# A transformer kernel on one core: the order of the dilated rounds, gates by tanh, normings of the sink layer on two engines, and a tile ahead of the norm roots

## Time and profile before

| | |
|---|---|
| median of three runs | 2550.37 us |
| profiled execution, device time | 2553.59 us |
| its span | 2551.8 us |
| PE busy | 2441.9 us, 96% |
| DVE, ACT, POOL busy | 1234.9, 984.5, 217.1 us |
| DMA queue of the weights | 206.55 MB, 25.4% of 16 engines |
| mean granted clock of PE | 0.975 |

### The profile page before, as it was taken

The page is one execution under the profiler, slowest core; times in us unless marked ns, Lnnn a source line. Parts: engine busy times, 40 slices in busy tenths (PEclk is TensorE's granted clock), DMA queues, the critical chain, the costliest instruction groups (busy, mean ns, idle before and its releaser), DMA issues.

```text
span 2551.8 us, 28618 instructions
## 1 busy us (share of the span) xinstructions
PE 2441.9 (96%) x11270; PEld 1947.0 (76%) x11270; DVE 1234.9 (48%) x2015; ACT 984.5 (39%) x1630; POOL 217.1 (9%) x161
## 2 busy tenths in 40 slices
PE   8999999999898999999998989999998879999998
PEld 6888877777776877888887667888886657888887
DVE  5533436788453436423337745424434755542433
ACT  4333223455343334322323554313324765431331
POOL 0101100322020100100100300000001220000000
PEclk9999999999998999999999989999998888999999
DMA  4223232111220232323322113322321102232221
GB/s 147 94 88 107 89 101 93 59 50 59 66 75 21 93 101 66 107 80 111 94 86 96 42 46 99 107 91 92 98 82 35 43 23 66 97 103 99 91 99 67
DMA packets 66903, 208.39 MB, mean 82 GB/s; under 512 B 7440, under 2 KB 16144, under 8 KB 66512
## 3 DMA queue, kind: packets, MB, share of 16 engines
q1 hardware_dynamic: 66768, 206.55, 25.4%
HBM read 204.42 MB, written 2.10 MB: 81 GB/s over the span
## 4 chain that ended last, share of the span: by engine, by line
PE 73%; issue 13%; DVE 5%; ACT 4%; POOL 4%; DMA 1%; POOLq 0%; SPq 0%; DVEq 0%; ACTq 0%
PE bank L1652 23%; PE bank L1656 22%; PE bank L1654 22%; POOL ftmps L2627 2%; POOL qk L2633 2%; PE bank L1787 1%; DVE wlo L2203 1%; ACT whi L1908 1%; DMA wraw<-in_stream 1%; PE bank L1778 1%; PE bank L1840 1%; PE bank L1714 0%; ACT tmps L2043 0%; PE bank L1724 0%; PE bank L1633 0%
## 5 line engine op out<-in xcount | busy, mean ns | idle before, releaser
L2203 DVE TENSOR_TENSOR wlo<-wraw,whi 128x1024 fp32r<-128x1024 f32 (+4 forms) x438 | 492.6, 1127 | 562.7 <-ACT whi L1908 561.4
L1652 PE MATMUL bank<-hhi,whi 128*128 128x512 f32 x1744 | 696.9, 400 | 13.5 <-ACT whi L1908 5.2
L1656 PE MATMUL bank<-hhi,wlo 128*128 128x512 f32 x1744 | 684.5, 392 | 1.8 <-DVE wlo L2203 1.6
L1654 PE MATMUL bank<-hlo,whi 128*128 128x512 f32 x1744 | 684.0, 392 | 1.7 <-DVE hlo L2209 1.7
L1908 ACT ACTIVATE whi<-wraw 128x1024 fp32r<-128x1024 f32 (+4 forms) x438 | 410.1, 937 | 509.7 <-PE bank L1656 448.0
L1652 PEld LDWEIGHTS bank<-hhi,whi 128*128 128x128 f32 x1744 | 330.0, 189 | 89.6 <-issue 13.5
L1656 PEld LDWEIGHTS bank<-hhi,wlo 128*128 128x128 f32 x1744 | 329.3, 189 | 76.2 <-DVE wlo L2203 5.7
L1654 PEld LDWEIGHTS bank<-hlo,whi 128*128 128x128 f32 x1744 | 330.2, 189 | 68.9 <-DVE hlo L2209 3.6
L1654 PE MATMUL bank<-mlo,whi 128*128 128x512 f32 x576 | 227.6, 395 | 0.2 <-DVE mlo L2460 0.2
L1652 PE MATMUL bank<-mhi,whi 128*128 128x512 f32 x576 | 227.6, 395 | 0.0
L1656 PE MATMUL bank<-mhi,wlo 128*128 128x512 f32 x576 | 227.5, 395 | 0.0
(11 more groups left out here) (381 smaller groups left out, 3145.6 us busy)
## 6 DMA issues: line engine op xcount, KB each, us to landing
wraw<-in_stream SPq DMA_DIRECT2D x343, 512.0 KB, 3.5
wraw<-in_stream SPq DMA_DIRECT2D x40, 192.0 KB, 2.4
wraw<-in_stream SPq DMA_DIRECT2D x22, 256.0 KB, 2.6
wraw<-in_stream SPq DMA_DIRECT2D x8, 320.0 KB, 2.9
xa<-in_x SPq DMA_DIRECT2D x8, 256.0 KB, 5.4
out<-ya SPq DMA_DIRECT2D x8, 256.0 KB, 2.6
m<-in_mask SPq DMA_DIRECT2D x1, 1024.0 KB, 4.8
wraw<-in_stream SPq DMA_DIRECT2D x8, 128.0 KB, 2.0
```

Source lines behind the costliest of these rows:

```text
L1652: pe.matmul(out, sh, xh, start=first, stop=False)
L1654: pe.matmul(out, sh, xl, start=False, stop=False)
L1656: p = pe.matmul(out, sl, xh, start=False, stop=end and last)
L2203: dve.tensor_tensor(wlo[j][:, 0:L], wraw[i][:, 0:L], whi[j][:, 0:L].bitcast(f32), SUB).then_inc(*lo.up(c))
```

## The change

- `DILATED_ORDER` gets gate tiles 4 and 5, `EARLY` is 6. Their results are kept in slots 6 and 7 of the q/k buffer, which the ring reaches last now (`QK` starts at slot 2), and which lies behind `m0`, `eb`, `m12`, `hc` in memory, clear of the merged tiles.
- The dilated loop has a round without a unit after each pair, with its fills times four; fills are 1.1, 1, 1, 0, 1 in a round.
- The gates use tanh of half the argument: ACT computes tanh(x/2), DVE multiplies by (1 + tanh), and the factor 0.5 is taken at the end, in the merged tile's high and low part.
- Sink layer: ACT norms the first half of a unit, DVE the second (`soft`), the turns wait for both. The order in a round is exp, score, output, fill 1.3, turns, fill 1.3, reciprocal and norming. Three of the first five pulls of filler come before the spread.
- FFN start: a third gate tile is run before the second `R.step()`, its `u` tile after the first two gates.
- `sums` with a spare bank begins with four more `keep_busy` matmuls, in all four norms.

```diff
-DILATED_ORDER = [("d", 1), ("a", 0), ("a", 1), ("d", 3), ("d", 5), ("a", 2), ("a", 3)]
-EARLY = 4
+DILATED_ORDER = [("d", 1), ("a", 0), ("a", 1), ("d", 3), ("d", 5), ("a", 2), ("a", 3), ("a", 4), ("a", 5)]
+EARLY = 6
...
                 g0, u0, g1, u1 = side_by_side(("h", s), *[(tag + c + "0", n, 0) for n in range(2) for c in "gu"])
+                g2 = run(feat([(tag + "g0", 2, 0)], ("h", s)))
                 R.step()
                 gate(s, 0, g0, u0, afree)
                 gate(s, 1, g1, u1, afree)
-                f = 2
+                gate(s, 2, g2, run(feat([(tag + "u0", 2, 0)], ("h", s))), afree)
+                next(extra, None)
+                f = 3
...
-    QK = Ring(range(8), guard)
+    QK = Ring([(i + 2) % 8 for i in range(8)], guard)
...
-                yield from gated_a(n, early[n], va_free)
+                if n >= 4:
+                    q = QK.take()
+                    assert q.i >= 6
+                    early.append(("qk", q.i))
+                yield from gated_a(n, early[n], va_free if n < 4 else q.was)
...
-    for unit in [dil_unit(p, i) for p in range(2) for i in range(4)] + [None]:
-        for l, fills in ((unit, 1.4), (last, 1.1), (last, 1.1), (last, 0), (unit, 1.1), (last, 0), (unit, 0)):
+    first, second = ([dil_unit(p, i) for i in range(4)] for p in range(2))
+    for unit in first + [None] + second + [None]:
+        pace = 1 if unit else 4
+        for l, fills in ((unit, 1.1), (last, 1), (last, 1), (last, 0), (unit, 1), (last, 0), (unit, 0)):
             if l:
                 next(l, None)
-            owed += fills
+            owed += fills * pace
...
     tv.freed(("ev_in", 0))
+    filler["gen"] = window_means()
+    fill(3)
     R.step()
...
-    filler["gen"] = window_means()
-    fill(5)
+    fill(2)
...
-        r.free = (("soft_act", ("even", u)),)
+        r.free = (("soft_act", ("even", u)), ("soft", ("even", u)))
...
-        for _ in turn("even", u, es, 2 * m, et, (("soft_act", ("even", u)),)):
+        for _ in turn("even", u, es, 2 * m, et, (("soft_act", ("even", u)), ("soft", ("even", u)))):
...
-           ((0, 0), (3, 0), (2, 1.3), (2, 0), (1, 1.3), (1, 0)))
+           ((1, 0), (0, 0), (3, 1.3), (2, 1.3), (1, 0), (1, 0)))
...
-            qk = sb("qk", [128, 8, S], where=ph)
             m0 = sb("m0", [128, 4, S], where=ph)
             eb = sb("eb", [128, 3072], where=ph)
             m12 = sb("m12", [128, 256], where=ph)
             hc = sb("hc", [128, 40], where=ph)
+            qk = sb("qk", [128, 8, S], where=ph)
...
                     waits(was)
+                    keep_busy(busy, 4)
                     for n, (where, tok) in enumerate(terms):
...
-                    for c in range(2):
-                        s = eb2[:, es, EW * c:EW * c + wd]
-                        p = act.activation(s, s, F.Copy, scale=SM(r, 6 + c))
-                    p.then_inc(*soft_act.up(("even", (n, i))))
+                    s = eb2[:, es, 0:wd]
+                    act.activation(s, s, F.Copy, scale=SM(r, 6)).then_inc(*soft_act.up(("even", (n, i))))
...
-                    act.activation(buf(where), buf(where), F.Sigmoid).then_inc(*ga_sig.up(n))
+                    act.activation(buf(where), buf(where), F.Tanh, scale=0.5).then_inc(*ga_sig.up(n))
...
-                    act.activation(mhi[:, n, :], buf(where), F.Copy).then_inc(*mg_hi.up(n))
+                    act.activation(mhi[:, n, :], buf(where), F.Copy, scale=0.5).then_inc(*mg_hi.up(n))
...
+                elif k == "even_soft":
+                    (n, i), es, r = a
+                    wd = (min(i + 2, 4) - max(i - 1, 0)) * 128
+                    s = eb2[:, es, EW:EW + wd]
+                    w.wait_ge(*recip["even", (n, i)])
+                    dve.tensor_scalar(s, s, SM(r, 7), None, MUL).then_inc(*soft.up(("even", (n, i))))
...
-                    dve.tensor_tensor(buf(where), buf(where), banks[b][:, :], MUL).then_inc(*pa_gated.up(n))
+                    dve.scalar_tensor_tensor(buf(where), buf(where), 1.0, banks[b][:, :], ADD,
+                                             MUL).then_inc(*pa_gated.up(n))
...
-                    dve.tensor_tensor(mlo[:, n, :], buf(where), mhi[:, n, :].bitcast(f32), SUB).then_inc(*mg_lo.up(n))
+                    dve.scalar_tensor_tensor(mlo[:, n, :], buf(where), 0.5, mhi[:, n, :].bitcast(f32), MUL,
+                                             SUB).then_inc(*mg_lo.up(n))
```

More of the change, by code:

```diff
@@ L1415, in buf @@
                 return eb[:, 512 * i:512 * i + 512]
-            return {"tmps": tmps, "ftmps": ftmps, "ssb": ssb, "mg": mg, "eb2": eb2, "eb3": eb3}[kind][:, i, :]
+            return {"tmps": tmps, "qk": qk, "ftmps": ftmps, "ssb": ssb, "mg": mg, "eb2": eb2, "eb3": eb3}[kind][:, i, :]
         def C(name, j=0, n=1):
@@ L2051, in scalar @@
                     w.wait_ge(*gb_scaled[n])
-                    act.activation(tmps[:, s2, :], tmps[:, s2, :], F.Sigmoid).then_inc(*gb_sig.up(n))
+                    act.activation(tmps[:, s2, :], tmps[:, s2, :], F.Tanh, scale=0.5).then_inc(*gb_sig.up(n))
                 elif k == "merge":
@@ L2457, in vector @@
                     waits(after)
-                    dve.tensor_tensor(tmps[:, s2, :], tmps[:, s2, :], banks[b][:, :], MUL).then_inc(*pb_gated.up(n))
+                    dve.scalar_tensor_tensor(tmps[:, s2, :], tmps[:, s2, :], 1.0, banks[b][:, :], ADD,
+                                             MUL).then_inc(*pb_gated.up(n))
                     w.wait_ge(*mg_hi[n])
-                    dve.tensor_tensor(mlo[:, n, :], buf(where), mhi[:, n, :].bitcast(f32), SUB).then_inc(*mg_lo.up(n))
+                    dve.scalar_tensor_tensor(mlo[:, n, :], buf(where), 0.5, mhi[:, n, :].bitcast(f32), MUL,
+                                             SUB).then_inc(*mg_lo.up(n))
                 elif k == "parts":
```

## The result

The changed kernel takes 2529.8 us in the median of four runs (2528.1 to 2530.9), the kernel before beside it 2550.9 (2548.1 to 2555.7): ratio 0.9915, interval 0.9898 to 0.9932. Forecast were 2527 and a range of 2518 to 2539. The profiled execution took 2529.56 us (span 2527.8), 24.0 less than that of before; the forecast's sum was 23.3. The medians lie 21.1 apart: the profiled execution of before took 2.7 us more than the median of these runs, that of after 0.3 less.

The account below looks back on a forecast made before the run. PE, busy 2441.9 of 2551.8 us, was taken as the bound, so only idle and low-clock time could be won. Terms 0.8 + 2.7 + 13.6 + 6.2 = 23.3 us gave 2527 us, range 2518 to 2539.

Parts of the forecast that it names:

- The dilated attention: Dilated attention stage: fewer turns without matmuls ahead and fewer waits for copies win 13.6 us, bounds 5 and 18.8.
- The count of pulls: Dilated rounds: 54 pulls leave four pieces without matmuls ahead, costing 4.0 of a 15.9 us loss; gain 11.9.
- the 4.4 us before (1,0): Dilated attention: PE's wait for the last rope before score (1,0) stays; no gain counted.
- The wait behind a norming in the first unit: Dilated attention, first unit: slower pace leaves 6 matmuls fewer ahead of a turn already waiting for DVE; -1.2 us.
- Tanh: Gates on ACT: eight table loads go in the dilated rounds; nothing counted, but the 13.6 would not hold without it.
- Rival 4: Dilated rounds: gates keep their table loads, six rounds wait 1.1 us each; 2533.7 us, chance 3%.
- The tile ahead of the FFN's root: Each FFN's start: one more gate tile covers PE's wait for the norm's root; gain 0.8 us, bounds 0 and 0.8.
- Four more fillers: Four norms' sums: clock holds after both FFNs, winning 4.5 us; the other two norms lose 1.8; sum 2.7.
- Rival 1: Norms: the fillers don't hold the clock, 2.7 us becomes -1.8; 2531.6 us, chance 15%.
- The sink layer: Sink layer: seven tail rounds win 6.7 us, residual 0.7, filled rounds 0.9; start loses 1.6, low clock 0.5; sum 6.2.
- Rival 2: Sink layer: late ropes and DVE normings behind POOL or masks eat the tail's gain; 2534.9 us, chance 13%.
- Rivals 3 and 5: 3: high clock in both attention tails, ready banks, 2520.6 us, 12%; 5: weight stream late for new tiles, 2573, 4%.

## Why the prediction was right

**The dilated attention, 13.6 forecast, 13.4 found.** The count of pulls was right to the piece: four turns or outputs wait for the copy, three in the last unit and one in (1,2), and the 4.4 us before (1,0) stay. The wait behind a norming in the first unit, priced at 1.2, cost 1.35. Of the 13.4 us only 6.1 are idle time, and those return in all nine profiles with this code. The clock's share came as forecast in six of the nine; in three it fell for longer at the 4.4 us and again behind the last turns, and the gain is 10.7 to 10.9. That the number is met to 0.2 us is luck to that extent. What the sum did not say is which edit earns it; the runs do: the two gates, 5.3 to 6.1 us of idle time, the loop 0 to 0.8. The 4.4 us that I gave up as staying were the cheapest thing to win: two pulls more in front of them.

**Tanh, 0 forecast, 0 found, but the reason beside it failed.** The sum held only "with" tanh, the prediction said, since 4.6 + 1.3 and a gate's own load are over 6. The run with sigmoid has the same stage to 0.01 us. My comparison put two loads into one gap between turns; but in eight rounds there are only six gates' functions on ACT, and only nine loads, so most gaps hold one load or none, and the waits of PE name ACT's copies of turns, not an exp behind a load. Rival 4 (loads kept, six rounds 1.1 later each) is refuted by its mechanism too: keeping the loads costs nothing.

**The tile ahead of the FFN's root, 0.8 forecast, 1.1 found.** The row that showed 0.84 us of idle time shows none at 1001.57.

**Four more fillers, 2.7 forecast.** The first norm did what was said: 380.27 to 386.27 is 6.00 us from the sums to the end of the spread, against 8.25. The step that failed is "if the clock then holds": after the second FFN it falls all the same (in the rows below the 14 records of fillers take 3.01 us, in the first norm 1.81), and in this profile 1.6 us of the first norm's gain went again at the next gap, where PE waits 1.83 us for the root; in nine of the twelve profiles with fillers they did not. PE, second norm:

```profile
1341.51 3.01 PE L1643 MATMUL bank<-ident,ones 128*128 128x128 f32 x14
1344.31 1.52 PE L1735 MATMUL bank<-ident,sm 128*128 128x128 f32 x8
```

The costs of 0.9 us in the other two norms came as worked out (0.8 and 0.7 net). A gain of 2.3 in one norm and up to 0.8 in another, less 1.5 in the two others, leaves 0.8 to 1.6, and nothing or less where the clock falls at the next gap. Rival 1 is half true. The 1.4 us of the stage table for the second norm are not the fillers', since the kernel without them has the same norm (9.54 us).

**The sink layer, 6.2 forecast, 9.9 found in the profiles, 12 when it is undone.** The start cost 1.8 us up to the first score, as forecast, with a low clock behind it. The mis-sized term is the tail. I took ACT's work, 2.2 to 2.7 us a turn and handovers, for the period, 2.9, and counted seven rounds at 3.86. The bare tail had six turns (1486.89 to 1506.76, 4.0 us apart), and in the changed kernel six follow at 2.5, 2.0, 2.8, 2.8 and 2.5 us, so it shrank by 8.1 us instead of 6.7, and the clock didn't fall in it, which gave the residual matmuls 2.0 us instead of 0.7. That last part is chance in one execution: in the profile of the sigmoid kernel, with this layer's code unchanged and the same gaps up to there, the clock fell in the tail, which took 18.8 us instead of 16.3, and the residual matmuls 24.5 instead of 22.5. Waits make 4.3 of the 9.9 us and come back; the clock's 5.6 vary, though the 12 us by which the medians lie apart when the layer is undone say that most of them are there in other executions too. The cause was mis-stated as well: the halved norming is worth 0.5 to 0.8 us; the order of the rounds carries 4.7 of the 5.2 us of waits that rounds and normings win together. Before, exps, normings and the turn that needs them stood in one chain within a round; now the norming (1480.40) is over when PE comes to the turn (1481.45), and exps of the next unit run meanwhile.

Rival 2, that normings on DVE wait for POOL, was true in its rows and false in its price. DVE's timeline, a norming beside a POOL multiply and one of the same size without:

```profile
1406.63 1.51 DVE L2430 TENSOR_SCALAR eb<-eb,sm 128x384 f32<-128x384 f32 x1
...
1410.03 0.42 DVE L2430 TENSOR_SCALAR eb<-eb,sm 128x384 f32<-128x384 f32 x1
```

The Trainium skill, "SBUF — State Buffer", section "Who interferes with whom", has the two exclude each other for a whole instruction; four of the sixteen normings show it (1.18 to 1.51 us), 0.8 to 1.1 us each. Undoing the split changes the median by less than a microsecond (2529.9 against 2529.8 and 2530.5), so these locks cost no more than the split wins.

**Rivals 3 and 5.** The dilated tail kept its clock in this profile; in others with the same code it falls once behind the last turns (from 839.11 in the kernel without fillers). The 2.5 us a round of rival 3 came in the sink layer alone. The weight stream held up nothing there: no wait for a DMA or for a weight split appears in the waits of PE between 690 and 845.

That the sum met the profile within 0.7 us owes something to errors of both signs: +3.7 in the sink layer, -2.4 in the norms and the value stage, and -0.7 behind the sink layer. It also owes something to this execution, the best of its kind in both attention stages. By the ratios of the runs, 0.9915 and 0.9914, the change wins 21.7 to 21.9 us, which is the fairer figure beside the forecast's 23.3.

## What to carry to other kernels

Count the filler pieces between the places where the matmul engine would otherwise wait; that count foretold the waits that were left, piece by piece, and also shows the next gain, since moving two pieces in front of a known wait won 6.5 us more. Compare two profiles by idle time and busy time apart: here the first came back within 0.1 to 1.8 us a stage and the second moved by up to 6.6 in code that hadn't changed. In a chain of small pieces over two engines, try the order in which one engine's queue holds them before moving work to another. An engine with more idle time than work between its deadlines takes 11.5 us of extra loads for nothing; look at what ended its idle time before its busy time is counted as a cost.

## What was not expected of the hardware

The granted clock is part chance. The same instructions, with the same gaps within 0.2 us, ran with a fall near 417 in three profiles and without it in nine, 1.6 us apart (67.1 to 67.3 us against 65.5 to 65.7 for the value stage); the norm ahead of it took 8.43 us in nine of the twelve with fillers and 9.24 to 9.29 in three. Where a program leaves a gap the fall may come at it, at the next one, or in neither. A forecast for a single gap's clock is then good to some 2 us, and a gain shown there in one profile is not yet a gain. Over a stage with many gaps it adds up: the sink layer, with the same code, took 161.3 to 167.2 us in seven profiles, with 6.8 to 23.9 us of it at the lower clock.
